# A decoder stack on one core: u and z from the input before its norm, the factor applied per four tiles, and the modulated norm's scale on VectorE in two of four groups

## The reference, cut to what matters

```python
def rmsnorm(x, g):
    y = x * lax.rsqrt(jnp.mean(x * x, axis=-1, keepdims=True) + RMS_EPS)
    return y * g

def s5_layer(h, ...):
    xn = rmsnorm(h, g_pre)
    u, z = jnp.split(xn @ w_in, 2, axis=-1)
    y = s5_ssm(u, ...)                       # linear in u
    y = jax.nn.gelu(y)
    y = y * jax.nn.sigmoid(y @ w_glu + b_glu)
    y = y * jax.nn.silu(z)
    return h + rmsnorm(y @ w_out, g_post)

def hybrid_layer(x, ...):
    h = rms_norm(x, g_norm) * (1.0 + scale) + shift
    proj = h @ w_in
    ...
```

## Time and profile before

| | |
|---|---|
| median of three runs | 3184.48 us |
| the profiled execution | 3182.76 us |
| its span in the trace | 3180.7 us |
| mean granted TensorE clock in it | 0.985 of full |
| instructions | 50285 |
| data moved | 645.74 MB, mean 203 GB/s |

### The profile page before, as it was taken

The page is one execution under the profiler, slowest core; times in us unless marked ns, Lnnn a source line. Parts: engine busy times, 40 slices in busy tenths (PEclk is TensorE's granted clock), DMA queues, the critical chain, the costliest instruction groups (busy, mean ns, idle before and its releaser), DMA issues.

```text
span 3180.7 us, 50285 instructions
## 1 busy us (share of the span) xinstructions
PE 3040.2 (96%) x20422; PEld 2651.7 (83%) x20422; DVE 2165.6 (68%) x2528; ACT 1513.8 (48%) x1911; POOL 108.3 (3%) x206
## 2 busy tenths in 40 slices
PE   6998998999999799999999999989999999999998
PEld 5898887877888688888888888878888888888887
DVE  7688777878765558667765667764755676655565
ACT  5454455334445534345455444453434545554444
POOL 0000000000000000000000000000000000000000
PEclk9999998999999999999999999999999999999999
DMA  6324675776544457646663477655754566445543
GB/s 220 121 107 146 219 255 217 274 260 231 205 172 172 158 203 280 243 176 218 233 229 135 183 284 267 230 192 186 276 185 159 194 231 237 146 166 219 186 173 131
DMA packets 103460, 645.74 MB, mean 203 GB/s; under 512 B 11616, under 2 KB 12640, under 8 KB 40160
## 3 DMA queue, kind: packets, MB, share of 16 engines
q1 hardware_dynamic: 71568, 508.12, 44.9%
q0 software_dynamic: 28528, 105.92, 9.2%
q10 hardware_dynamic: 3168, 28.84, 2.2%
HBM read 628.15 MB, written 14.68 MB: 202 GB/s over the span
## 4 chain that ended last, share of the span: by engine, by line
PE 80%; DVE 11%; ACT 5%; issue 3%; DMA 1%; DVEq 0%; ACTq 0%; POOLq 0%
PE acc L1879 40%; PE acc L1881 20%; PE acc L1840 7%; DVE wlo L1059 3%; PE acc L1874 3%; ACT whi L511 2%; DVE xs L1191 2%; PE acc L1876 1%; DVE modacc L1087 1%; DVE s5c L1253 1%; PE bank L2024 1%; PE bank L2205 1%; PE bank L2228 1%; DVE w L1253 1%; DMA modw<-in_modstream 1%
## 5 line engine op out<-in xcount | busy, mean ns | idle before, releaser
L1879 PE MATMUL acc<-xs,whi 128*128 128x512 f32 x6192 | 2208.9, 401 | 65.4 <-DVE xs L1191 50.4
L1881 PE MATMUL acc<-xs,wlo 128*128 128x256 f32 x6192 | 1740.4, 281 | 0.0
L1879 PEld LDWEIGHTS acc<-xs,whi 128*128 128x128 f32 x6192 | 1169.1, 189 | 356.6 <-issue 36.5
L1059 DVE TENSOR_TENSOR wlo<-raw,whi 128x2048 fp32r<-128x2048 f32 x451 | 1033.5, 2292 | 495.5 <-ACT whi L511 494.6
L1881 PEld LDWEIGHTS acc<-xs,wlo 128*128 128x128 f32 x6192 | 1175.9, 190 | 1.0
L511 ACT ACTIVATE whi<-raw 128x2048 fp32r<-128x2048 f32 x451 | 860.2, 1907 | 119.5 <-PE acc L1840 119.5
L547 ACT ACTIVATE acctmp<-acc 128x256 f32<-128x256 f32 x387 | 148.3, 383 | 967.7 <-PE acc L1881 956.6
L1128 DVE TENSOR_TENSOR w<-acc,acctmp 128x256 f32<-128x256 f32 (+1 forms) x352 | 152.3, 433 | 330.5 <-ACT acctmp L547 330.0
L1840 PE MATMUL acc<-whi,xs 128*128 128x512 f32 x768 | 242.1, 394 | 10.1 <-DVE w L1120 7.0
L1087 DVE SCALAR_TENSOR_TENSOR modacc<-modw,cact,modacc 128x1024 f32<-128x1024 f32 x180 | 230.2, 1279 | 7.5 <-DMA modw<-in_modstream 7.0
L1840 PEld LDWEIGHTS acc<-whi,xs 128*128 128x128 f32 x768 | 145.7, 190 | 44.7 <-issue 13.7
(11 more groups left out here) (301 smaller groups left out, 2332.6 us busy)
## 6 DMA issues: line engine op xcount, KB each, us to landing
raw<-in_wstream SPq DMA_DIRECT2D x479, 1024.0 KB, 4.8
modw<-in_modstream POOLq DMA_DIRECT2D x192, 512.0 KB, 4.4
residual<-h ACTq DMA_DIRECT2D x2, 2048.0 KB, 10.9
ga_gate<-w ACTq DMA_DIRECT2D x2, 2048.0 KB, 10.7
gated_retention<-w ACTq DMA_DIRECT2D x2, 2048.0 KB, 9.4
h<-gated_retention ACTq DMA_DIRECT2D x2, 2048.0 KB, 11.0
h<-residual ACTq DMA_DIRECT2D x2, 2048.0 KB, 10.4
ga_w<-ga_gate ACTq DMA_DIRECT2D x8, 512.0 KB, 9.9
```

The lines of the kernel that those rows point to most:

```text
L1059: dve.tensor_tensor(out=wlo[s % SPL][:, :], in0=raw[s % RAW][:, :], in1=whi[s % SPL][:, :].bitcast(F32), op=ALU.subtract).then_inc(w_lo_do ...
L1879: pe.matmul(acc[par % 2][0:cols, :], whi[w][:, c:c + cols], x_split[:, k, :, :], start=(k == 0), stop=False, skip_group_check=True)
L1881: mm = pe.matmul(acc[par % 2][0:cols, 0:T], wlo[w][:, c:c + cols], x_split[:, k, 0, :], start=False, stop=(k == kts - 1), skip_group_check ...
```

## The change

It has two parts. In the S5 layer, x is only scaled by `norm_pre0` (into `w2`) and split; u and z are computed from it, and the factor comes later. The squares are taken in place in `h` after ScalarE's second weight split, folded by VectorE after tiles 1 and 2, summed by TensorE ahead of its side work of tile 3, and the factor is spread at the end of that side work. VectorE multiplies u by it four tiles at once after tiles 3, 7, 11 and 15, and TensorE's `ends` waits for that. z is multiplied in the first four tiles of glu; the sigmoids move to tiles 1, 2, 5, 7 and the products to tiles 4, 6, 7, 10. The small tensors are loaded ahead of x, and ScalarE scales and splits group 0 ahead of the sines. In the modulated norm, groups 1 and 3 get their scale together with the factor from VectorE in four instructions, ScalarE adds the shift and rounds in one, and VectorE adds the shift again while it subtracts.

```diff
 MID_KNOWN = 6
+Z_GATE_AT, Z_USED_AT = (1, 2, 5, 7), (4, 6, 7, 10)
+SHIFT_LATE = (1, 3)
...
 def _(sp):
     sp.dma_start(adt[:, :, :], s5_adt).then_inc(sem("adt_loaded"), 16)
-    for g in range(4):
-        sp.dma_start(h[:, 4 * g:4 * g + 4, :], x_p[:, 4 * g:4 * g + 4, :]).then_inc(x_loaded[g], 16)
...
         sp.dma_start(dst, src).then_inc(params_loaded, 16)
+    for g in range(4):
+        sp.dma_start(h[:, 4 * g:4 * g + 4, :], x_p[:, 4 * g:4 * g + 4, :]).then_inc(x_loaded[g], 16)
...
 def _(pool):
...
     pool.memset(ones_1[:, :], 1.0).then_inc(sem("ones_set"), 1)
-    pool.wait_ge(x_lo_done, SPLIT_BEFORE["pre0"] + 4)
+    pool.wait_ge(sem("pre0_folded"), 2)
...
             act.wait_ge(sem("norm_scaled"), 4 * (name == "pre_l1") + g + 1)
+            if g in SHIFT_LATE:
+                act.wait_ge(acc_done, JOBS[(0 if name == "pre_l0" else 1, "rq")][1])
+                for k in range(4):
+                    i = 4 * g + k
+                    last = act.activation(xs[:, i, 0, :], stg_half(g)[:, k, :], ACT.Identity, bias=mv[:, i:i + 1])
+                    if k == 2:
+                        last.then_inc(x_staged, 1)
+                last.then_inc(x_hi_done, 1)
+                continue
...
     act.activation(sm[2][:, :], sm[1][:, :], ACT.Exp).then_inc(sem("s5_mag"), 1)
+    def scaled_x(g):
+        act.wait_ge(x_loaded[g], 16)
+        for k in range(4 * g, 4 * g + 4):
+            last = act.activation(w2[:, k, :], h[:, k, :], ACT.Copy, scale=vcol("norm_pre0")(k))
+        last.then_inc(x_staged, 1)
+        split_x("pre0", group(w2), xs, 0, (g,))
+    act.wait_ge(params_loaded, 64)
+    scaled_x(0)
...
+    scaled_x(1)
+    split_hi(0, 0)
+    scaled_x(2)
+    scaled_x(3)
+    split_hi(1, 1)
     for g in range(4):
-        act.wait_ge(x_loaded[g], 16)
-        act.activation(group(w1)(g), group(h)(g), ACT.Square).then_inc(sem("pre0_square"), 1)
-    act.wait_ge(params_loaded, 64)
-    act.wait_ge(sem("pre0_square"), 4)
-    for k in range(KT):
-        last = act.activation(h[:, k, :], h[:, k, :], ACT.Copy, scale=vcol("norm_pre0")(k))
-        if k % 4 == 3:
-            last.then_inc(sem("x_scaled"), 1)
-    root("pre0")
-    split_hi(0, 0)
-    split_x("pre0", stg_half, xs, 0)
-    split_hi(1, 1)
+        act.activation(group(h)(g), group(h)(g), ACT.Square).then_inc(sem("pre0_square"), 1)
...
     def take_e(g):
...
         take_b(g, 2 * i + 1)
+        if j == 3:
+            root("pre0")
...
     def glu_side(j):
...
-        if j < 4:
-            if j >= 2:
-                act.wait_ge(sem("z_used"), j - 1)
-            act.activation(stg_half(j), group(w2)(j), ACT.Sigmoid).then_inc(sem("z_gate"), 1)
-        elif j % 4 == 0:
+        if j in Z_GATE_AT:
+            g = Z_GATE_AT.index(j)
+            act.wait_ge(sem("z_scaled"), g + 1)
+            if g >= 2:
+                act.wait_ge(sem("z_used"), g - 1)
+            act.activation(stg_half(g), group(w2)(g), ACT.Sigmoid).then_inc(sem("z_gate"), 1)
+        if j and j % 4 == 0:
...
     def gated_early():
...
                     dve.wait_ge(x_lo_done, SPLIT_BEFORE[name] + g - 1)
-                tt(stg_half(g), group(src)(g), bcast(spread_rstd(name), 4), ALU.mult).then_inc(sem("norm_scaled"), 1)
+                if g in SHIFT_LATE:
+                    for k in range(4):
+                        i = 4 * g + k
+                        ins = dve.scalar_tensor_tensor(out=stg_half(g)[:, k, :], in0=src[:, i, :], scalar=gsc[:, i:i + 1],
+                                                       in1=spread_rstd(name), op0=ALU.mult, op1=ALU.mult)
+                    ins.then_inc(sem("norm_scaled"), 1)
+                else:
+                    tt(stg_half(g), group(src)(g), bcast(spread_rstd(name), 4), ALU.mult).then_inc(sem("norm_scaled"), 1)
...
                 split_held((0, "out") if l else (None, "foxout"))
-            if g >= 1:
+            if g - 1 in SHIFT_LATE:
+                dve.wait_ge(x_hi_done, SPLIT_BEFORE[name] + g)
+                for k in range(4):
+                    i = 4 * (g - 1) + k
+                    ins = dve.scalar_tensor_tensor(out=xs[:, i, 1, :], in0=stg_half(g - 1)[:, k, :],
+                                                   scalar=modv[l][:, i:i + 1], in1=xs[:, i, 0, :].bitcast(F32),
+                                                   op0=ALU.add, op1=ALU.subtract)
+                ins.then_inc(x_lo_done, 1)
+            elif g >= 1:
...
     def add_normed(src, total, after=lambda g: None):
...
     reduce_angle(S[5], S[3], S[6], True).then_inc(sem("s5_reduced"), 1)
+    def pre0_lo(g):
+        dve.wait_ge(x_staged, STAGED_BEFORE["pre0"] + g + 1)
+        split_x("pre0", group(w2), xs, g)
+    def pre0_fold(part):
+        folded = sem("pre0_folded")
+        if part == 0:
+            dve.wait_ge(sem("pre0_square"), 4)
+            for g in range(2):
+                tt(group(h)(g), group(h)(g), group(h)(g + 2), ALU.add).then_inc(folded, 1)
+            return
+        dve.wait_ge(folded, 2)
+        tt(group(h)(0), group(h)(0), group(h)(1), ALU.add).then_inc(folded, 1)
+        for n in (2, 1):
+            dve.wait_ge(folded, 5 - n)
+            tt(h[:, 0:n, :], h[:, 0:n, :], h[:, n:2 * n, :], ALU.add).then_inc(folded if n == 2 else sq_done, 1)
+    pre0_lo(0)
...
     dve.wait_ge(sem("s5_sincos"), 1)
-    half = lambda a: w1[:, 2 * a:2 * a + 2, :]
-    for g in range(1, 4):
-        dve.wait_ge(sem("pre0_square"), g + 1)
-        link(tt(group(w1)(0), group(w1)(0), group(w1)(g), ALU.add))
-    tt(half(0), half(0), half(1), ALU.add).then_inc(sq_done, 1)
...
-    rms("pre0")
+    pre0_lo(1)
     split_lo(0, 0)
-    for g in range(5):
-        if g < 4:
-            dve.wait_ge(sem("x_scaled"), g + 1)
-            if g >= 2:
-                dve.wait_ge(x_lo_done, SPLIT_BEFORE["pre0"] + g - 1)
-            tt(stg_half(g), group(h)(g), bcast(rstd[:, :], 4), ALU.mult).then_inc(x_staged, 1)
-        if g:
-            split_x("pre0", stg_half, xs, g - 1)
+    pre0_lo(2)
+    pre0_lo(3)
...
     def complex_mul(w, x, same, cross):
...
             dve.wait_ge(sem("s5_w3"), g)
-        else:
-            dve.wait_ge(x_lo_done, SPLIT_BEFORE["pre0"] + 4)
...
             tt(shift[:, 1:NCH], ident[:, 0:NCH - 1], ident[:, NCH:2 * NCH - 1], ALU.add).then_inc(sem("shift_set"), 1)
+        if j == 3:
+            dve.wait_ge(sq_used, 1)
+            dve.tensor_scalar(ms[:, :], bank[0][:, 0:2], 256 / OVER["pre0"], EPS, ALU.mult, ALU.add).then_inc(ms_ready, 1)
+            dve.wait_ge(ms_rooted, 1)
+            dve.reciprocal(ms[:, :], ms[:, :]).then_inc(rstd_ready, 1)
         if j == 15:
+            dve.wait_ge(acc_summed, j + 1)
+            tt(group(w1)(g), group(w1)(g), bcast(rstd[:, :], 4), ALU.mult).then_inc(sem("u_scaled"), 1)
...
             next_power(g, 2)
+            if j == 1:
+                pre0_fold(0)
...
             next_power(g, 3)
+            if j == 2:
+                pre0_fold(1)
...
             next_power(g + 1, 1)
+        if j == 3:
+            dve.wait_ge(sem("rstd_spread"), 1)
+            link(dve.tensor_copy(rstd[:, :], bank[0][:, T:2 * T]))
+        if i == 3 and j < 15:
+            dve.wait_ge(acc_summed, j + 1)
+            tt(group(w1)(g), group(w1)(g), bcast(rstd[:, :], 4), ALU.mult).then_inc(sem("u_scaled"), 1)
     project((None, "u"), lambda j: tile(w1, j), side=u_side)
...
     def glu_mul(g):
         dve.wait_ge(sem("glu_gate"), g + 1)
+        dve.wait_ge(sem("z_used"), g + 1)
...
     def glu_side(j):
...
         if j < 4:
-            dve.wait_ge(sem("z_gate"), j + 1)
-            link(tt(stg_half(j), stg_half(j), group(w2)(j), ALU.mult))
-            tt(group(w1)(j), group(w1)(j), stg_half(j), ALU.mult).then_inc(sem("z_used"), 1)
-        if j == 4:
-            dve.wait_ge(sem("z_used"), 4)
+            if j == 0:
+                dve.wait_ge(acc_summed, JOBS[(None, "glu")][1])
+            tt(group(w2)(j), group(w2)(j), bcast(rstd[:, :], 4), ALU.mult).then_inc(sem("z_scaled"), 1)
+        if j in Z_USED_AT:
+            g = Z_USED_AT.index(j)
+            dve.wait_ge(sem("z_gate"), g + 1)
+            link(tt(stg_half(g), stg_half(g), group(w2)(g), ALU.mult))
+            tt(group(w1)(g), group(w1)(g), stg_half(g), ALU.mult).then_inc(sem("z_used"), 1)
...
     def gated_lo(g):
...
-    def spread(name):
+    def spread(name, to=bank[4]):
...
         for m in range(2):
-            mm = pe.matmul(bank[4][:, m * P:(m + 1) * P], ms[:, m:m + 1].to_broadcast([P, P]), ident[:, :],
+            mm = pe.matmul(to[:, m * P:(m + 1) * P], ms[:, m:m + 1].to_broadcast([P, P]), ident[:, :],
...
     pe.wait_ge(sem("ones_set"), 2)
-    pe.wait_ge(sq_done, 1)
-    for k in range(2):
-        for m in range(2):
-            mm = pe.matmul(bank[0][:, m:m + 1], w1[:, k, m * P:(m + 1) * P], part[:, 0:1], start=(k == 0 and m == 0),
-                           stop=(k == 1), skip_group_check=True)
-    mm.then_inc(sq_used, 1)
     pe.wait_ge(params_loaded, 64)
-    spread("pre0")
...
```

(11 more changed lines are left out.)

## The result

The changed kernel takes 3198.59 us as the median of nine runs (3188.28 to 3209.45), the kernel before 3184.48 (nine runs, 3176.89 to 3191.97): ratio 1.0046, 95% interval 1.0032 to 1.0060, 14 us slower. The forecast, 3185.5 with 3174 to 3194, is missed, and by more than the range allows.

The account below looks back on a forecast made before the run. TensorE, busy 96% of the span, was taken as the bound. Terms -8.4 + 6.5 + 2.4 + 0 + 0.5 = +1.0 on the profiled 3182.8 gave 3183.8, or 3185.5 us as a median; range 3174 to 3194.

Parts of the forecast that it names:

- the start: Before the first matmul: norm work removed, small loads ahead of x; first matmul at 20.9 instead of 27.5, gain 8.4 us.
- tile 3: Where the mean goes: TensorE waits 2.1 for folds and 3.3 before the spread, plus sums and spread; loss 6.5 us.
- Rival 3: At the start, x lands late or ScalarE's order starves the constants: +2 to +4, 3187 to 3189 us; chance 0.06.
- The table load: Sine table on ScalarE's path at the start: 1.28 us, with the skill's 1.38 drain left outside the sum.
- rival 2: Clock falls at tile 3's waits, so spread and block 4 cost 0.6 + 2.8 more: +4.4, 3189 us; chance 0.12.
- The factor on u: One product per group after the next power; TensorE waits 1.2 before end states of groups 1 and 2; loss 2.4 us.
- Rivals 1 and 4: First: tile 3's mean costs TensorE only 1.1, total 3180 us, chance 0.20. Other: norms gain 2, about 3183 us, chance 0.04.
- The factor on z: In glu, four more VectorE products replace pairs moved to later tiles: no effect, bounds 1.2 us either way.
- the modulated norms: VectorE's scale work in groups 1 and 3 takes longer: loss 0.5 us for both norms, bounds 2 gained, 1.5 lost.

Follow-up runs that it names:

- the two waits alone: Kernel before the change plus a product-sized VectorE operation on u of groups 1 and 2, for which `ends` waits: 3194.33 us, ratio 1.0031.
- the two repairs: Two edits of the changed kernel: u product of groups 1 and 2 ahead of the next power (3183.08 us); mean worked out one tile earlier (3184.94 us).
- one wait: Kernel before the change plus the added VectorE operation on u of group 1 only, for which `ends` waits: 3190.01 us, ratio 1.0013.
- both repairs: Changed kernel with the u product ahead of the next power and the mean one tile earlier: 3180.18 us, ratio 0.9977.
- the mean early: Changed kernel with squares folded one tile earlier and mean, root and reciprocal in the side work of tile 2: 3184.94 us, ratio 0.9999.
- the product first: Changed kernel with VectorE multiplying u of groups 1 and 2 before the next group's power: 3183.08 us, ratio 1.0002.
- half waits: Kernel before the change plus a VectorE operation on two tiles of u, not four, for which `ends` of groups 1 and 2 waits: 3199.49 us, ratio 1.0045.

## Why the prediction was wrong, point by point

- **In sum.** The terms other than the clock came to +1.0 in the prediction and to -0.2 (2.4 either way) in the table above. That is a little luck, since the start gained 2.0 more than forecast and tile 3 lost 1.5 more. What the sum put at nothing is the clock behind the new waits, and the clock took 15.9.
- **The start: right in kind, 2 us better than forecast.** First matmul forecast at 20.9, measured 19.88; block 1 at 30.2 against 28.12 (before 38.56), so 10.4 were gained at that point, not 8.4. x landed earlier than taken: the first scaling starts at 7.58 behind an issue at 3.21, where the sum had 9.0. Block 0 took 7.5 (19.88 to 27.34), not 8.3. Rival 3 fell.
- **The table load** costs its 1.28 and no more. In the chain the copy ends at 10.38, the load starts at 10.39 and ends at 11.67, the sine starts at 11.69. The drain of 1.38 us that the Trainium skill names (ScalarE: Activation LUTs, section What ACT_TABLE_LOAD costs) doesn't show on either side of it, so the measurement decides for leaving it out.
- **Tile 3: the two waits right to 0.1 us** (2.1 and 3.3 forecast; 2.1 and 3.2 measured), and so were the sums (0.5; 0.61). The loss between blocks 4 and 6 was 8.0 and not 6.5: the spread took 1.22 and not 0.6, block 4 began at 0.64 per pair, the two together some 1.5 us. So the clock part of rival 2 did happen here, at about half of its price of 3.4 in this profile. Over all executions the two stops are dearer: the repair that shortens them brings back 5 us of waits and 10 of clock.
- **The factor on u: the step that failed.** It said: "For group 1 that power ends at 104.6 and TensorE starts the end states at 104.57: the whole 1.2 is a new wait; the same for group 2 … Loss 2.4; bounds 0 and 3." The waits were there, 1.35 each, 2.7 in all. What the step lacked is what such a wait does to the clock of the 256 matmuls behind it, a term it put at nothing: in the kernel before the two waits alone cost 10 us (ratio 1.0031), and one fall is 6.6 of them. The bound should have reached to two falls, 2.7 + 2 x 6.6 = 15.9.
- **Rival 2 had the mechanism and denied it the place.** "For a verdict of slower it would have to happen five times, and there is one place." There are three: tile 3 and both waits ahead of `ends`. It took the earlier trace rows, where the clock held through 2.94 us of idle time, for a threshold in the length of the wait; but the waits of the table of falls, less than half as long, let it fall in 10 of 17 cases. And the fall was priced at 2.8 for a block of eight pairs; behind `ends` it costs 6.6, since `ends` itself loses 4 to 5. The Trainium skill, TensorE: Matmul & The Clock Gate, Part 1, has half rate as the default and full rate as what activity earns; the window of the changed kernel (0.73 behind a wait of 1.35) agrees with that. Why so short a wait is enough in some executions and not in others, no run here shows. It gave this rival 0.12 and put it at +4.4; the time is of its kind at three times its size.
- **Rivals 1 and 4** fell: TensorE did stop at tile 3, and the norms gained nothing.
- **The factor on z and the modulated norms: right.** In the stretch of glu the distance between the kernels stays within 2 us of where it was, and the norms as before change nothing (1.0045 against 1.0046). TensorE's wait for the low half of group 2, forecast near 3, was 2.1 in the first profile and 2.9 in the third.

The account of the changed kernel up to block 15, from its second profile, the one with both falls: start -10.5, tile 3 with its clock about +9, group 1 +8.1 (from 1.4 ahead at block 6 to 6.7 behind at block 11), group 2 +8.1; 14.7 behind at block 15. The two waits and the two falls are more than all that the start gains.

Open: the effects of the two repairs don't quite add. Each alone brings back 14 to 15 us, both together 18 (3198.6 to 3180.2). If they added, the changed kernel would stand at 1.0002 + 0.9999 - 0.9977 = 1.0024, and it stands at 1.0046; the intervals just allow it. By the estimate above the waits add (2.9 and 5.1 against 7.5) and what doesn't is the clock. It fits the table of falls that the clock falls at the first wait ahead of `ends` in the four profiles that stood at tile 3 before, and at the second in the four with two such waits of 1.34 us that hadn't; but one profile of the latter had a stop of 2.9 us at 37 us too, and in the kernel with one wait the clock fell at the first without any stop at tile 3, so that is a pattern and not shown. A wait ahead of large matmuls was not added by itself; the one of 1.17 ahead of block 1 says that the clock can fall there too, in two of six profiles, for 3.4 us instead of 13.7, which cost the two kernels some 1.5 us.

## What to carry to other kernels

Price a new wait of TensorE by what stands behind it, not by its length alone: here 1.3 us ahead of 256 small matmuls took the clock down in 10 of 17 cases and then cost six times its length (8.0 for 1.34). Halving the wait didn't make the kernel faster, though no profile has a fall at the shorter waits; having none did. It need not be small matmuls that stand behind it, but the two falls behind a wait of 1.17 ahead of large ones lasted a quarter as long. Where VectorE has two things to do, the one that TensorE will want first goes first, even when both are done "in time": here one swap of two operations was worth 15 us. And when a gain from one part (a start 10 us earlier) doesn't arrive, look for it before giving the change up: with the waits out of the way 4 us of it stayed in the median, 7 by the ratio.

## What the runs showed of the hardware that was not expected

- The fall of the clock is a matter of chance from one execution to the next, at a fixed place. The same kernel had one fall or two in the u stage, and its nine runs spread over 21 us, those of the kernel with both repairs over 11. A single profile can be the luckiest run (here it was, 10 us under the median), so the median's difference can't be read from one trace.
- A stop of TensorE with no releaser, in the midst of the small matmuls of `kernels` (bank<-cbd,wgen, ahead of the last 19 of them) at about 36 us in the kernels with the early start: 0.8 us in one profile and 2.9 in the other of the same kernel with the mean early. In the changed kernel it was 0.6, 0.4 and 1.3; in the profile with both repairs there is none. The clock fell behind the stops of 2.9 and 3.0 us (the second is that of the product first) and behind no shorter one; in the two profiles with the mean early it was 1.00 and 0.86 in the window 36 to 60 us:

```profile
36.00:60.00 24.00, 22.17 (x320) 19.29 (x306) 22.79 (x27) 11.62 (x22) 2.65 (x4) 1.00 0.66 236
```

```profile
36.00:60.00 24.00, 20.10 (x342) 17.47 (x330) 17.63 (x22) 10.91 (x20) 2.65 (x4) 0.86 0.47 169
```

  The low half of block 4 started at 45.84 in the first and 51.10 in the second. The profiles with one wait and with half waits have such a stop too, at about 48 us (1.5 and 2.3 us), and so has the product ahead of the next power, at 37 us (3.0); the profile of the kernel before has none. The program has no wait at this place, and what it is isn't known from these traces. It is a second place where the falls of some executions may come from, those of the half wait above all; its seven executions lost 10 us more to the clock than the kernel before, by the estimate above.
